# The router between the last mixer and the experts: weights brought earlier, 16-column split, whole row tiles, first item's rows by counted token numbers, a list by broadcast

## The reference

```python
xn = _rmsnorm(x, W['norm_ffn_g'][i])
...
logits = jnp.dot(xt.astype(jnp.float32), w_router.astype(jnp.float32))   # 1024 -> 8 experts
top_v, top_i = lax.top_k(logits, TOP_K)                                  # two experts a token
top_w = jax.nn.softmax(top_v, axis=-1)
flat_e = top_i.reshape(-1)
order = jnp.argsort(flat_e)                                              # pairs sorted by expert
tok = order // TOP_K
xs = xt[tok]
sizes = jnp.bincount(flat_e, length=N_EXPERTS)
h = jax.nn.silu(lax.ragged_dot(xs, wg, sizes)) * lax.ragged_dot(xs, wu, sizes)
ys = lax.ragged_dot(h, wd, sizes) * top_w.reshape(-1)[order][:, None]
y = jnp.zeros_like(xt).at[tok].add(ys)
```

## Time and profile before

| | us |
|---|---|
| runs | 5119.39, 5131.51, 5133.02 |
| median | 5131.51 |
| profiled execution, its time | 5134.26 |
| profiled execution, span of its trace | 5132.7 |
| last product of `w_out` issued in layer 1 | 2609.55 |
| first product of the first expert item | 2702.35 |

### The profile page before, as it was taken

One profiled execution on the slowest core, in us unless ns is written; L12 is line 12 of the kernel. 1 busy time (PEld: TensorE's weight loads), 2 busy tenths in 40 slices (PEclk: granted clock), 3 DMA queues, 4 the chain that ended last, 5 costly groups with the idle time before them and its releaser, 6 DMA issues. The chain is left out here.

```text
span 5132.7 us, 86754 instructions
## 1 busy us (share of the span) xinstructions
PE 4942.7 (96%) x33110; PEld 4876.0 (95%) x33111; DVE 3395.0 (66%) x5288; ACT 1597.7 (31%) x2290; POOL 396.3 (8%) x239
## 2 busy tenths in 40 slices
PE   8999999999999999999969999999999999999968
PEld 8999999999998999999959999999999999999968
DVE  5677757444556756876557777666667777876665
ACT  2112122111113311122224444333334444443333
POOL 3110101110102021110010000000000000000020
PEclk9999999999999999999979999999999999999989
DMA  3111111111111111111035554444446555654431
GB/s 105 44 45 41 41 40 42 50 41 44 46 41 44 41 56 40 47 41 42 29 117 177 177 175 165 160 146 160 150 148 207 187 192 184 199 185 150 146 125 42
DMA packets 398841, 527.64 MB, mean 103 GB/s; under 512 B 11944, under 2 KB 353494, under 8 KB 398504
## 3 DMA queue, kind: packets, MB, share of 16 engines
q1 hardware_dynamic: 359552, 460.75, 27.3%
q0 software_dynamic: 10912, 33.94, 2.0%
q10 hardware_dynamic: 28040, 28.63, 1.7%
HBM read 494.87 MB, written 28.39 MB: 102 GB/s over the span
## 5 line engine op out<-in xcount | busy, mean ns | idle before, releaser
L1596 DVE TENSOR_TENSOR WLO<-WRAW,WHI 128x1024 fp32r<-128x1024 f32 x866 | 1071.3, 1238 | 340.8 <-ACT WHI L1192 215.9
L658 PE MATMUL PS<-XHI,WHI 128*128 128x384 f32 (+1 forms) x3648 | 1203.2, 330 | 10.6 <-DVE XLO L1843 4.5
L660 PE MATMUL PS<-XHI,WLO 128*128 128x384 f32 (+1 forms) x3648 | 1197.6, 328 | 0.0
L659 PE MATMUL PS<-XLO,WHI 128*128 128x384 f32 (+1 forms) x3648 | 1197.1, 328 | 0.0
L1192 ACT ACTIVATE WHI<-WRAW 128x1024 fp32r<-128x1024 f32 x866 | 899.1, 1051 | 892.2 <-PE PS L773 602.8
L658 PE MATMUL PS<-XSH,WHI 128*128 128x232 f32 (+6 forms) x3584 | 1058.3, 295 | 12.5 <-DVEq L2300 12.2
L659 PE MATMUL PS<-XSL,WHI 128*128 128x232 f32 (+6 forms) x3584 | 1054.7, 294 | 0.0
L660 PE MATMUL PS<-XSH,WLO 128*128 128x232 f32 (+6 forms) x3584 | 1054.6, 294 | 0.0
L658 PEld LDWEIGHTS PS<-XHI,WHI 128*128 128x128 f32 x3648 | 691.7, 190 | 13.0 <-issue 5.2
L658 PEld LDWEIGHTS PS<-XSH,WHI 128*128 128x128 f32 x3584 | 678.7, 189 | 14.4 <-DVEq L2300 13.8
L659 PEld LDWEIGHTS PS<-XLO,WHI 128*128 128x128 f32 x3648 | 691.4, 190 | 0.9
(11 more groups left out here) (361 smaller groups left out, 5956.6 us busy)
## 6 DMA issues: line engine op xcount, KB each, us to landing
WRAW<-in_moe_w_gate SPq DMA_DIRECT2D x112, 1024.0 KB, 5.0
WRAW<-in_moe_w_up SPq DMA_DIRECT2D x112, 1024.0 KB, 5.0
WRAW<-in_moe_w_down SPq DMA_DIRECT2D x112, 1024.0 KB, 5.0
WRAW<-in_w_in SPq DMA_DIRECT2D x48, 1024.0 KB, 5.2
WRAW<-in_ffn_w_gate SPq DMA_DIRECT2D x11, 1024.0 KB, 5.2
WRAW<-in_ffn_w_up SPq DMA_DIRECT2D x11, 1024.0 KB, 5.3
WRAW<-in_ffn_w_down SPq DMA_DIRECT2D x11, 1024.0 KB, 4.9
XG<-sorted_rows POOLq DMA_DIRECT2D x18, 512.0 KB, 4.6
```

The source lines that it names most:

```text
L658: pe.matmul(PS[:, bank, 0:n], wh, hi(k), start=(k == 0), stop=False)
L659: pe.matmul(PS[:, bank, 0:n], wh, lo(k), start=False, stop=False)
L660: ins = pe.matmul(PS[:, bank, 0:n], wl, hi(k), start=False, stop=(k == KC - 1))
L1596: v.do(dve.tensor_tensor(WLO[s][:], raw_view(conv.n // 2 % RAW, conv.n % 2, kind), WHI[s][:].bitcast(F32), ALU.subtract), conv)
```

## The change

`RW`'s load and its split move into the `w_out` projection: POOL issues it once layer 1's mixers have been evicted (`Q_MIX1`), and DVE splits it after column 3 of `w_out`. The split now stands in one tile of 16 columns, `RWS` (8 of the high half, 8 of the low), so a channel block takes two products in place of three; the two partial sums come out on 16 partitions and are added by the turn to token rows, with `TWIN` (two unit matrices stacked) in place of the unit matrix. `XF` goes: PE makes token rows from `XHI` and `XLO` directly, 144 products in place of 72. `YT` as row buffer goes: nine buffers `ROWT` lie over memory of the items, and ACT also writes each to a new DRAM tensor `token_rows`. DVE and PE make from the counts the token numbers of the first item's rows (`MASK`, `IDS`), and POOL gathers these rows from `token_rows` into `XG`; the 18 scatters to `sorted_rows`, and three writes behind its last row that stood ahead of them, come after the gathers. ACT and DVE wait for the scatters later, where they write over `ROWT`. The list is made with fewer and wider instructions. On PE, ACT and DVE a branch passes over the extra items' loop.

```diff
# gpsimd
-        g.wait_ge(S["phase_clear"], 1)
+        g.wait_ge(S["evicted"], Q_MIX1)
         g.dma_start(RW[:], A["router_w"][0].rearrange("(k p) e -> p k e", p=P)).then_inc(S["rw_loaded"], 16)
...
+        g.wait_ge(S["rows_written"], 16 * NT)
+        g.wait_ge(S["ids_ready"], 1)
+        for c, (r0, n) in enumerate(XBLK):
+            g.indirect_dma_start(XG[0:n, c, :], None, XR[0:NTOK, :], bass.IndirectOffsetOnAxis(ap=IDS[0:n, c:c + 1], axis=0)).then_inc(S["xg_ready"], 16)
         for j, (r0, n) in enumerate(XBLK):
-
-            g.dma_start(XS[PAIRS + r0:PAIRS + r0 + n, :], XG[0:n, j, :]).then_inc(S["scattered"], 16)
+            g.dma_start(XS[PAIRS + r0:PAIRS + r0 + n, :], ROWT[j][0:n, :]).then_inc(S["scattered"], 16)
+        g.wait_ge(S["places_ready"], 1)
         for j in range(NT):
...
-                g.indirect_dma_start(XS[0:PAIRS, :], bass.IndirectOffsetOnAxis(ap=POSI[0:n, k, j:j + 1], axis=0), YT[j % 3][0:n, :],
-                                     None).then_inc(S[f"rows_gone{j % 3}"], 16)
+                g.indirect_dma_start(XS[0:PAIRS, :], bass.IndirectOffsetOnAxis(ap=POSI[0:n, k, j:j + 1], axis=0), ROWT[j][0:n, :],
+                                     None).then_inc(S[f"rows_gone{j // 3}"], 16)
...
-        for j, (r0, n) in enumerate(XBLK):
-            g.dma_start(XG[0:n, j, :], XS[bass.ds(row + r0, n), :]).then_inc(S["xg_ready"], 16)
# tensor
+                def logits(j):
...
+                    t0, n = BLOCKS[j]
+                    b = misc_bank()
+                    for k in range(KC):
+                        if k in (0, KC - 1):
+                            pe.wait_ge(S["split_done"], W_MOE - 3 + (j + 1 if k else 0))
+                        hi = lambda **f: pe.matmul(PS[0:2 * NE, b, 0:n], RWS[:, k, :], XHI[:, k, t0:t0 + n], **f)
+                        lo_ = lambda: pe.matmul(PS[0:NE, b, 0:n], RWS[:, k, 0:NE], XLO[:, k, t0:t0 + n], start=False, stop=False)
...
+                            for X in (XHI, XLO):
+                                ins = pe.matmul(PS[0:n, b, k * P:(k + 1) * P], X[:, 4 * h + k, j * P:j * P + n], IDR[:], start=(X is XHI), stop=(X is XLO))
...
+                logits(0)
+                logits(1)
+                stats()
+                logits(2)
+                rows(0)
                 pe.wait_ge(S["logits_ready"], 1)
...
+                for j in range(1, 5):
                     rows(j)
                 pe.wait_ge(S["counts_ready"], 1)
...
+                for j in range(5, NT):
                     rows(j)
+                b = misc_bank()
+                for j in range(NT):
+                    n = tokens(j)
+                    pe.wait_ge(S["mask_ready"], j + 1)
+                    for c in (0, 2, 1):
...
+                        ins = pe.matmul(PS[0:w, b, c:c + 1], MASK[0:n, j, r0:r0 + w], ONES[0:n, 0:1], start=(j == 0 and c == 0),
+                                        stop=(j == NT - 1 and c == 1))
# scalar
+                act.wait_ge(S["scale_ready"], 1)
                 for j in range(NT):
                     n = tokens(j)
-                    if j == 0:
-                        act.wait_ge(S["counts_ready"], 1)
-                    if j >= 3:
-                        act.wait_ge(S[f"rows_gone{j % 3}"], 32 * (j // 3))
...
-                    act.sem_inc(S["rows_ready"], 1)
+                    act.dma_start(XR[j * P:j * P + n, :], ROWT[j][0:n, :]).then_inc(S["rows_written"], 16)
...
+                act.br_lt(extras, 1, on_true="act_firsts", on_false="act_further").branch_hint(further)
...
                 for k in range(KC):
                     prepare(k)
+                act.wait_ge(S["rows_gone0"], 96)
+                act.wait_ge(S["pads_clear"], 1)
# vector
-                for j in range(1, NT + 1):
-                    v.do(dve.tensor_tensor(CS[:, j, :] if j < NT else TM[:, 0, :], CS[:, j - 1, :], SS[:, j - 1, :], ALU.add))
+                for part in (CS, TM, CS, TM):
...
+                for j in range(NT):
+                    v.do(dve.tensor_scalar(MASK[:, j, :], RANKS[:], C0[:, j:j + 1], None, ALU.is_ge), masked)
...
-                for size in SIZES[:-1]:
-                    v.do(dve.tensor_scalar(lrow(PLACE), lrow(SIZE), size + 0.5, None, ALU.is_ge))
-                    v.sync()
-                    v.do(dve.tensor_tensor(lrow(OTHER), lrow(OTHER), lrow(PLACE), ALU.add))
-                    v.sync()
+                v.do(dve.tensor_tensor(LCMP[:], lrow(SIZE).unsqueeze(2).to_broadcast([1, NJ, n_levels]),
+                                       LEVEL[:].unsqueeze(1).to_broadcast([1, NJ, n_levels]), ALU.is_gt))
...
                 for r, out in ((EXPERT, 0), (ROW, 1), (SIZE, 2)):
-                    v.do(dve.tensor_tensor(LSEL[:], wide(lrow(b)), SLI[:].unsqueeze(2).to_broadcast([1, SLOTS, NJ]), ALU.is_equal))
+                    v.do(dve.tensor_tensor(LPICK[:], LSEL[:], wide(lrow(r)), ALU.mult))
...
-                for i in range(3):
-                    dve.wait_ge(S[f"rows_gone{i}"], 32 * (NT // 3))
-                v.do(dve.memset(EACC[:], 0.0))
```

More of the change, by code:

```diff
@@ L2234, in _ @@
-                for p_ in range(1, EXTRA + 1):
-                    v.do(dve.tensor_scalar(further(ACTIVE, p_), CNT[0:1, :], CAP * p_ + 0.5, None, ALU.is_ge))
-                    v.do(dve.tensor_copy(further(EXPERT, p_), IOT[0:1, :]))
-                    v.do(dve.tensor_scalar(further(ROW, p_), BASE[0:1, :], float(CAP * p_), None, ALU.add))
-                v.do(dve.memset(firsts(ACTIVE), 1.0))
-                v.do(dve.tensor_copy(firsts(EXPERT), IOT[0:1, :]))
+                every = lambda t: t.unsqueeze(2).to_broadcast([1, NE, EXTRA])
@@ L2353, in _ @@
                 first, second, *middle, late, last = list(groups(MOE_GROUPS))
-                with dve.Fori(0, SLOTS - NE) as it:
-                    with dve.If(it < extras):
-                        st = looped(cs, it, per)
-                        kp[0] = LOOK
-                        for k in range(KC):
-                            prepare(k)
-                        step(*first)
-                        step(*second, between=lambda u: item_out(it, u) if u < len(XBLK) else None)
-                        for s in (*middle, late, last):
-                            step(*s)
-                        leave_items(cs, st, per, extras)
+                dve.br_lt(extras, 1, on_true="dve_firsts", on_false="dve_further").branch_hint(further)
+                with nc.body("dve_further", valid_engines=[dve.engine]):
+                    with dve.Fori(0, SLOTS - NE) as it:
+                        with dve.If(it < extras):
+                            st = looped(cs, it, per)
+                            kp[0] = LOOK
+                            for k in range(KC):
+                                prepare(k)
+                            dve.wait_ge(S["rows_gone0"], 96)
+                            dve.wait_ge(S["pads_clear"], 1)
+                            step(*first)
+                            step(*second, between=lambda u: item_out(it, u) if u < len(XBLK) else None)
+                            for s in (*middle, late, last):
+                                step(*s)
+                            leave_items(cs, st, per, extras)
+                    dve.br("dve_firsts")
+                nc.switch_bb("dve_firsts")
                 for k in range(KC):
                     prepare(k)
+                dve.wait_ge(S["rows_gone0"], 96)
+                dve.wait_ge(S["pads_clear"], 1)
                 with dve.Fori(0, NE) as e:
```

270 lines of the change are left out of this document (166 added, 104 removed).

## The result

| | before | after |
|---|---|---|
| median of 15 runs | 5129.93 us | 5145.33 us |
| lowest and highest | 5119.39, 5135.98 | 5135.61, 5151.22 |
| profiled execution, span | 5132.7 | 5149.2 |
| last `w_out` product issued | 2609.55 | 2609.33 |
| first product of the first item | 2702.35 | 2714.90 |

The ratio is 1.0029, with a 95% interval of [1.0022, 1.0036]: the change makes the kernel 15 us slower, where 10 us of gain were forecast. The trace puts 12.8 us of it in the gap and 0.4 in the first item; the other 2 to 4 are within what two single executions differ by. The next five items last as long as before (1382.7 us, before 1382.5, by POOL's loads of rows).

The account below looks back on a forecast made before the run. Bound: TensorE's 92.5 us gap before the first item. Third conversion 2678.5 + 1.06 + branch 1 + 11.3 = 2691.9 against 2702.35, gain 10.4: median 5131.51 - 10.4 = 5121.1 us; range 5107 to 5132.

Parts of the forecast that it names:

- What bounds the kernel: TensorE's standstill between `w_out` and the first item: 92.5 us is the whole stake; third conversion sets the product's earliest start.
- Logits: Directly behind `w_out`, with `RW` split earlier: `LG` near 2623.0 in place of 2635.75, 12.7 us won.
- Counts: From `LG` to `CNT`, TensorE doing row tiles 1 to 4 first (7.7 us): `CNT` at 2632.4, 10.5 us won.
- Token numbers: Between `CNT` and places: masks 3.2 us, 27 TensorE products 4.8 us; `IDS` at 2640.1, 4.4 us won.
- List: From places to `ITEMS`: 9.9 us in place of 18.0, `ITEMS` at 2651.1, 12.5 us earlier.
- Rows: ACT's writes, then POOL's gathers: first item's rows in `XG` before 2652, 38 us earlier, no longer deciding.
- Weights: First weight tiles beside scatters, 85 against 310 GB/s: third conversion at 2678.5 in place of 2681.26; the deciding term.
- Shares by bytes: Rival, chance 0.21: weights and POOL's queue get equal bytes, weights at 194 GB/s; gain 20.5 us, 5111.
- The tail: Rival, chance 0.12: both queues move 13.8 MB at 294 GB/s, ending at 2690; nothing won, 5132.
- Slower by the instruction stream: Rival, chance 0.04: TensorE's longer program brings instructions late in each item; 80 us over eight items gives 5201.
- 30 us of slip, and I give it no case of its own: Gathers landing after 2680, so that the first item's rows still decide, would take 30 us of slip; no chance given.
- POOL starts its gathers much later than 2642: Sign that the forecast is wrong: late gathers in the gap would give the weights a free queue; no size given.

Follow-up runs that it names:

- e12: Changed kernel with four idle 384-column products ahead of each half of a row tile, 72 in all, on TensorE; 5151.56 us in one run.
- e7: Changed kernel with 13 idle copies of 448 elements ahead of `ITEMS` on VectorE, so the list comes later; 5142.44 us, 1.0029 of the kernel before.
- e10: Changed kernel with the two weight tiles of each item's first step read in 4 KB runs, not 1 KB; 5133.36 us, 1.0010 of the kernel before.
- e2: Changed kernel with VectorE reading the token numbers `IDS` after the list is written; 5119.82 us, 0.9982 of the kernel before.
- e9: Changed kernel, TensorE order tiles 1-2, counts, tiles 3-8, mask products in fp32r; token numbers read after the list; 5113.94 us, 0.9973 of the kernel before.
- e4: Changed kernel with the logits' high products holding 128 weight columns in place of 16; 5145.20 us, 1.0033 of the kernel before.
- e14: e9 with two idle 384-column products ahead of each half of a row tile, scatters directly behind the gathers; 5127.85 us, 0.9998 of the kernel before.
- e11: Changed kernel without token numbers and `token_rows`, first item's rows loaded from `sorted_rows`, counts behind tile 2; 5122.47 us, 0.9988 of the kernel before.

## Why the prediction was wrong

**What bounds the kernel**: right. The gap was the stake, the item code did not move (259.7 and 260.0), and the third conversion, the table load and the 11.3 us behind it set the product. The branch cost nothing (0 us where 1 was taken).

**Logits**: right. `LG` at 2623.51 for 2623.0. Inside the term sizes were off and partly cancelled: `stats` took 1.98 us for 2.4 and the logits' end came at 2619.4 for 2620.4; the turn took 2.15 for 0.7, since the fp32 products with `TWIN` are two instructions each (x18 for nine) where the transposes of before were one (x9).

**Counts**: the first step that failed. The term "row tiles 1 to 4 first, 64 x 0.12 = 7.7 us" took 13.4: each product stepped by 0.21, because the clock fell to 1.2 GHz at 2623.7. The step of 0.12 had been read at 2.4 GHz, and the text counted on it without asking what would keep the clock; a busy engine seemed enough. `CNT` came at 2638.17 for 2632.4, 5.8 us late. The Trainium skill (TensorE: Matmul & The Clock Gate, Part 1) says that the gate is set by how busy the array has been of late. If busy is what the profile calls busy, the trace disagrees: TensorE is busy in all of 20.00 us and the clock fell, and it stayed up only with wide products between (e12).

**Token numbers**: the step with the largest error, `IDS` at 2660.34 for 2640.1. VectorE's part was right (4.9 us for 5.3). On TensorE, tiles 5 to 8 ended only at 2649.97, 15.3 us behind the 2634.7 of the text: 5.8 came with `CNT`, and the text had let their 64 products pass for about 2 us (they took 12.0, and 7.7 even at its own 0.12). Then the mask products: "27 one-column products at 3.18/18 = 0.18, 4.8 us". The 18 in that row are instructions of 9 products. 27 fp32 products are 54, and took 10.3. This step and the one before are where the prediction failed: a chain on TensorE that was priced at 15 us (7.7 + 2.3 + 4.8) took 36 (13.4 + 12.0 + 10.3), and list and gathers both hang on its end.

**List**: its length was right (9.4 us for 9.9). Its start was not, for VectorE reads `IDS` ahead of the places. So `ITEMS` came at 2671.20 for 2651.1, 7.6 later than before where 12.5 earlier was forecast.

**Rows**: they landed long before they were needed, but POOL's queue started at 2661.5 and not at 2642.

**Weights**: the mechanism was right, in every part that could be tested: equal packets (532 and 533), bytes as 3.6 to 1 (forecast 310 to 85 GB/s), the end set by the sum of the bytes and hardly by the list (e7). From the first gather 13.8 MB at 387 GB/s are 35.7 us: 2661.5 + 35.7 = 2697.2, measured 2702.5. So of the 24 us by which the third conversion was late, 18.5 (2661.5 for 2643) are the late start, and 5.3 that the 2.1 MB were not through at the full rate. Of these the trace shows 1.5 before the first byte moved (2663), 2 from 2663 to 2674, where q0 alone moved 3.47 MB, 316 GB/s, and some 2 at the end, when 0.9 MB of the third weight tile (q1 moved 3.01 MB from 2661 to 2703) went through before the last of the second; the rates between, 405 to 412 GB/s, took a little back.

**The rivals.** Shares by bytes: refuted by the same counts. The Trainium skill (DMA: Bandwidth & Descriptors, SWDGE vs HWDGE vs iDMA) has an engine change queues only between packets, and prefers packets up to 4096 bytes. The equal counts agree with the first, and with 4 KB packets the gap was 11 us shorter (e10). That the 1 KB runs would be bundled to such packets, the text's own "if", did not happen. The tail: 5.3 us of this kind came about; in the other 18 it has no part. Slower by the instruction stream: refuted (the first item 260.0 for 259.7, the next five 1382.7 for 1382.5). The slower outcome that came about was not among the rivals: **the chain of TensorE ahead of counts and token numbers** was worked into the sum with quick sizes, and the one rival of that kind ("30 us of slip, and I give it no case of its own") looked only at the rows and not at the list that hangs on the same wait. The text named the sign ("POOL starts its gathers much later than 2642") and drew the wrong end of it: the weights got no free queue, since the list slipped as far as the gathers.

**The range** came from what stands behind the list alone: the conversion, the branch, and the two rivals on the queues. (The bounds of 5114 to 5128 are missummed: 4 us of conversion and 1 of branch off 5121.1 give 5116.) What stands ahead of the list went in with one value each, and row tiles and mask products had no bound on the late side, though the low clock was in the text ("a granted clock of 0.50", "`stats` took 3.18 at the low clock"). With the measured sizes put in, 13.4 + 12.0 + 10.3, the same sum gives about 5140, within 6 us of the measured time.

## What to carry to other kernels

Price what stands ahead of a wait on the in-order engine at both clocks and by instructions, not by products, and let the range reach to the dearer end. When a new result is read by an engine that has a longer chain to feed, read it last: e2 is worth 25 us with the same work; e9, which also shortens the chain, 31. And where two queues meet, ask which is there first and how large its packets are; when both start together, only their bytes count, and 1 KB packets beside 4 KB ones get a fifth of the rate.

## What the runs showed of the hardware

- TensorE's clock fell from 2.4 to 1.2 GHz while it was busy all the time, 4 us behind the last of the logits' 320-column products and 14 behind the last of `w_out`, in turns of 8 columns and row pieces of 128. Holding 128 columns in the logits did not keep it (e4), nor did two products of 384 columns to eight short ones (e14); four did (e12), and 72 additional products then cost nothing.
- Beside POOL's queue, with about 3.6 KB a packet, SP's queue with 1 KB moved 0.53 MB in 6 us against 1.94; with 4 KB, 1.22 against 1.19. Alone it moved 2.10 MB within 11 us. Its first packet showed 4 us behind the issue beside the full queue, 1 us without it.
- The medians of e11 and e14 stand 7 us above what gap and item of their traces give against the kernel before; for the other kernels it is 4 us at most. Their traces are of executions that took 4.6 us (e11) and 13.2 us (e14, its fastest) less than the median, so they may not show what the median holds; that stays open.
